# The up products of the feed-forward and gated blocks: 256-column low-weight products alternate with 512-column ones

## What is computed

```python
def conv_glu_ffn(h, w_in, conv_w, conv_b, w_out):      # twice ("ffn")
    gate, val = split(h @ w_in)                        # 1024 -> 2 x 2816
    gate = conv3_along_tokens(gate, conv_w) + conv_b
    return (gelu(gate) * val) @ w_out                  # 2816 -> 1024

def swiglu(x, w_gate, w_up, w_down):                   # twice ("glu")
    return (silu(x @ w_gate) * (x @ w_up)) @ w_down
```

## Time and profile before

| | us |
|---|---|
| median of 3 runs | 1209.4 |
| lowest, highest | 1207.72, 1209.48 |
| the profiled execution, first to last instruction | 1208.0 |
| TensorE busy | 1189.8 (98%) |
| TensorE weight loads | 1038.1 (86%) |
| VectorE busy | 939.8 (78%) |
| ScalarE busy | 667.1 (55%) |
| GpSimd busy | 150.4 (12%) |
| busy share of the DMA queue with the weights | 52.2% |

### The profile page before, as it was taken

How to read it: one execution, slowest core, us unless ns; L and a number is a source line. 1 busy time by engine, 2 the same in 40 slices (tenths; PEclk the granted TensorE clock), 3 DMA queues, 4 the chain that set the end, 5 groups by cost and what they waited for, 6 DMA issues and landing times.

```text
span 1208.0 us, 17902 instructions
## 1 busy us (share of the span) xinstructions
PE 1189.8 (98%) x6979; PEld 1038.1 (86%) x6979; DVE 939.8 (78%) x1270; ACT 667.1 (55%) x1060; POOL 150.4 (12%) x275
## 2 busy tenths in 40 slices
PE   8999999999999999999999999999999999999997
PEld 7898888888889988888888988888897888888886
DVE  6767898888776679989887889777775968667765
ACT  5665654444767776544447755434676555444445
POOL 5300510000200012000002100000208420000002
PEclk9999999999999999999999999999999999999999
DMA  7847386555544445665555565655455146565540
GB/s 245 254 154 232 137 269 209 177 196 170 187 151 150 132 149 200 209 206 178 193 170 185 183 230 182 201 178 170 147 175 174 36 156 211 183 209 184 200 140 36
DMA packets 151640, 215.84 MB, mean 179 GB/s; under 512 B 6970, under 2 KB 116924, under 8 KB 151556
## 3 DMA queue, kind: packets, MB, share of 16 engines
q1 hardware_dynamic: 148092, 207.46, 52.2%
q0 software_dynamic: 1760, 3.94, 1.2%
q10 hardware_dynamic: 1704, 3.28, 0.8%
HBM read 213.60 MB, written 1.06 MB: 178 GB/s over the span
## 4 chain that ended last, share of the span: by engine, by line
PE 91%; DVE 4%; ACT 2%; issue 1%; POOL 1%; DMA 0%; POOLq 0%; ACTq 0%; DVEq 0%
PE work L2408 24%; PE work L2411 13%; PE acc L1996 10%; PE acc L1997 9%; PE acc L1998 9%; PE work L1996 5%; PE work L1998 5%; PE work L1997 5%; DVE w_lo L1298 1%; PE work L2397 1%; PE work L2385 1%; PE work L2399 1%; PE work L2018 1%; PE work L2526 1%; PE acc L2053 1%
## 5 line engine op out<-in xcount | busy, mean ns | idle before, releaser
L1298 DVE TENSOR_TENSOR w_lo<-raw,w_hi 128x2048 fp32r<-128x2048 f32 (+1 forms) x194 | 440.7, 2278 | 60.6 <-ACT w_hi L719 60.6
L719 ACT ACTIVATE w_hi<-raw 128x2048 fp32r<-128x2048 f32 (+2 forms) x193 | 365.2, 1898 | 69.5 <-PE work L2411 60.1
L2408 PE MATMUL work<-hT_both,w_hi 128*128 128x512 f32 x1280 | 318.8, 391 | 0.0
L2408 PEld LDWEIGHTS work<-hT_both,w_hi 128*128 128x128 f32 x1280 | 234.8, 188 | 45.2
L2411 PEld LDWEIGHTS work<-hT_both,w_lo 128*128 128x128 f32 x1280 | 174.6, 190 | 12.5
L2411 PE MATMUL work<-hT_both,w_lo 128*128 128x256 f32 x1280 | 178.5, 282 | 0.0
L1996 PE MATMUL acc<-w_hi,aux_hi 128*128 128x512 f32 x400 | 157.8, 395 | 0.0
L1997 PE MATMUL acc<-w_lo,aux_hi 128*128 128x512 f32 x400 | 156.7, 392 | 0.0
L1998 PE MATMUL acc<-w_hi,aux_lo 128*128 128x512 f32 x400 | 155.8, 390 | 0.0
L1085 ACT ACTIVATE aux_hi<-Z 128x256 fp32r<-128x256 f32 x88 | 36.9, 419 | 195.8 <-DVE Z L1722 107.8
L1693 DVE TENSOR_REDUCE Z<-work 128x256 f32<-128x512 f32 x88 | 60.6, 689 | 90.2 <-PE work L2411 88.5
(11 more groups left out here) (271 smaller groups left out, 1782.4 us busy)
## 6 DMA issues: line engine op xcount, KB each, us to landing
raw<-in_ffn_w_in SPq DMA_DIRECT2D x44, 1024.0 KB, 5.2
raw<-in_ffn_w_out SPq DMA_DIRECT2D x22, 1024.0 KB, 5.0
raw<-in_w_gate SPq DMA_DIRECT2D x22, 1024.0 KB, 5.3
raw<-in_w_up SPq DMA_DIRECT2D x22, 1024.0 KB, 5.3
raw<-in_w_down SPq DMA_DIRECT2D x22, 1024.0 KB, 5.0
raw<-in_na_w_qkv SPq DMA_DIRECT2D x12, 1024.0 KB, 7.5
raw<-in_da_w_qkv SPq DMA_DIRECT2D x12, 1024.0 KB, 5.3
raw<-in_ple_w_gate SPq DMA_DIRECT2D x8, 1024.0 KB, 5.0
```

The lines of the kernel that those rows point to most:

```text
L719: act.activation(w_hi[:, n % RING, 0:size], raw[:, n % RAW, 0:size], ACT.Copy).then_inc(hi_done, 1)
L1298: dve.tensor_tensor(w_lo[:, n % RING, 0:size], raw[:, n % RAW, 0:size], w_hi[:, n % RING, 0:size].bitcast(F32), ALU.subtract).then_inc(lo_ ...
L2408: pe.matmul(b.rearrange("p (e s) -> p e s", e=2), v[0][:, k, cols(c % 2)], hT_both[:, k, :, :], start=k == 0, stop=False)
```

## The change

A constant `LAG = 4` is added and `up` is written anew. The products, their operands and banks are the same, and so are their number and the order of k within a kind. What is new is the order: after four big products of half 0, each further big product is followed by a small one, four steps behind it. The last four small products of half 0 stand between the first four big ones of half 1; the last four of half 1 stand alone at the end. So one call goes: 4 big, 12 pairs of big and small, 4 small. Before a half's first big product the wait is now for `hi_done`; that for `lo_done` comes before the half's first small product. The bank of half 0 is full after half 1's fourth big product, that of half 1 at the end as before.

```diff
--- before.py
+++ after.py
@@ -63,6 +63,7 @@
 N_EARLY = 56
 N_CONV = 3 * FT + FT
 EARLY_UP = FT - 4
+LAG = 4
 RELOAD = 16
 
 
@@ -1997,10 +1998,13 @@
                 pe.matmul(dst, stationary[0], moving[1], start=False, stop=False)
                 return pe.matmul(dst, stationary[1], moving[0], start=False, stop=last)
 
+            def slab_views(n):
+                k, c = slabs[n][1:3]
+                return [r[:, n % RING, 0:k * c].rearrange("p (k n) -> p k n", k=k) for r in (w_hi, w_lo)]
+
             def slab(n):
                 pe.wait_ge(lo_done, n + 1)
-                k, c = slabs[n][1:3]
-                return [r[:, n % RING, 0:k * c].rearrange("p (k n) -> p k n", k=k) for r in (w_hi, w_lo)]
+                return slab_views(n)
 
             def both(pair, *at):
                 return [v[at] for v in pair]
@@ -2400,17 +2404,39 @@
                                             start=False, stop=last)
                             if last:
                                 ins.then_inc(bank_full[(up_bank(ph, c) + i) % WORK], 1)
+                def up_part(ph, c, i, part, k):
+                    g, v = up_bank(ph, c) + i, slab_views(b0 + 3 * (c // 2) - (c >= 2) + i)
+                    d = work[:, g % WORK, :]
+                    if part == 0:
+                        return pe.matmul(d.rearrange("p (e s) -> p e s", e=2), v[0][:, k, cols(c % 2)],
+                                         hT_both[:, k, :, :], start=k == 0, stop=False)
+                    ins = pe.matmul(d[:, 0:S], v[1][:, k, cols(c % 2)], hT_hi[:, k, :], start=False, stop=k == KT - 1)
+                    if k == KT - 1:
+                        ins.then_inc(bank_full[g % WORK], 1)
+                    return ins
+
                 def up(c):
                     g, n = up_bank(ph, c), b0 + 3 * (c // 2) - (c >= 2)
-                    for i in range(2):
-                        v, b = slab(n + i), open_bank(pe, g + i)
-                        for k in range(KT):
-                            pe.matmul(b.rearrange("p (e s) -> p e s", e=2), v[0][:, k, cols(c % 2)], hT_both[:, k, :, :],
-                                      start=k == 0, stop=False)
-                        for k in range(KT):
-                            ins = pe.matmul(b[:, 0:S], v[1][:, k, cols(c % 2)], hT_hi[:, k, :],
-                                            start=False, stop=k == KT - 1)
-                        ins.then_inc(bank_full[(g + i) % WORK], 1)
+                    pe.wait_ge(hi_done, n + 1)
+                    open_bank(pe, g)
+                    for k in range(KT):
+                        up_part(ph, c, 0, 0, k)
+                        if k == LAG:
+                            pe.wait_ge(lo_done, n + 1)
+                        if k >= LAG:
+                            up_part(ph, c, 0, 1, k - LAG)
+                    pe.wait_ge(hi_done, n + 2)
+                    open_bank(pe, g + 1)
+                    for k in range(KT):
+                        up_part(ph, c, 1, 0, k)
+                        if k < LAG:
+                            up_part(ph, c, 0, 1, KT - LAG + k)
+                        if k == LAG:
+                            pe.wait_ge(lo_done, n + 2)
+                        if k >= LAG:
+                            up_part(ph, c, 1, 1, k - LAG)
+                    for k in range(KT - LAG, KT):
+                        up_part(ph, c, 1, 1, k)
 
                 def down(c, ts=range(T)):
                     v = slab(b0 + min(3 * (c // 2) + 4, 3 * STEPS - 1))
```

## The result

The changed kernel takes 1214.0 us (median of 5 runs, 1212.36 to 1214.68) against 1209.48 for the kernel before (5 runs, 1207.72 to 1210.15). The ratio is 1.0041, 95% interval 1.0028 to 1.0053: slower by 4.5 us, where 0.3 us less was forecast (1209.1). The profiled execution spans 1212.1 us, 4.1 more than the 1208.0 of before.

A forecast was written before the change was run, and what follows sets the result against it. TensorE's own pace was taken as the bound; -0.8 us from the order of products and +0.5 us at the ffn block ends gave -0.3 us, 1209.1 us against 1209.4. Own range 1207 to 1211.8, 8 in 10 1202.4 to 1214.9.

The forecast's parts named there:

- What bounds the kernel: Whole kernel: TensorE busy 98% of the span and, inside the wide layers, waiting for nobody.
- Part 1, the pace of the pairs: Order of products in up: a call takes 5.570 us, 0.010 less, times 80 calls -0.8 us.
- P: Time of one big and one small product alternating in up: 0.347 us taken, bounds 0.340 and 0.353 to 0.356.
- its sign of being wrong: In the 12 pairs of a call: P leaving 0.345 to 0.350 us would show the forecast wrong.
- the prediction's own sum: One call of up: 1.406 + 12 P us, including 0.02 that small products leave behind.
- the 5.58 that stands for before: One up in the kernel before: 5.56 us, 5.58 with what it leaves in the down.
- No cover to be had: Weight loads in up: by the skill's rule 107 ns, just fitting behind 256 columns, so alternation has nothing to cover.
- The equal 0.013 us over the columns: Big and small products: both exceed columns at 2.4 GHz by 0.013 us, read as a fixed price of changing weights.
- The loads are covered: Rival, pairs in up: small products take 0.113 us, P = 0.340, -7.0 us in all, 1202.4 us; chance 0.32.
- Part 2, the waits: Separate waits for w_hi and w_lo in up: looser wait gives nothing, earlier need fits 1.95 us lead; 0 us.
- Part 3, the late bank: Gate half's bank full 0.93 us later: 0 mid-block, 0 to 0.25 us per ffn block end, +0.5 us taken for two.
- each change of kind costs: Rival, big product in the 12 pairs: a debt at every change, P = 0.353, 1214.9 us; chance 0.23.

The follow-up runs named there:

- e1: Kernel before with test stretches on TensorE behind the stored result, of one width or mixed; only starts count: 512 with 256 columns one by one took 353 ns a pair.
- e2: Kernel before, its product order kept, with the changed kernel's waits for hi_done and lo_done: 1208.16 us against 1209.42, ratio 0.9994.
- e9: Changed kernel with two big and two small products at a time in place of one and one: 1208.67 us against 1208.02 for the kernel before, ratio 1.0001.
- e4: Kernel before with big and small products alternating within each half, small one step behind, old waits, bank 0 full at its old place: 1213.68 us against 1209.42.
- e3: Kernel before with all 16 big products of a call first, then all 16 small ones: 1210.3 us against 1209.42, ratio 1.0005.
- e6: Kernel before with two big, two small products in turn within each half, old waits: 1208.6 us against 1209.52, ratio 0.9993.
- e7: Kernel before with a second test stretch behind the stored result: more widths, mixtures and group sizes; only starts count: 512 with 272 columns took 360 ns a pair.

## Why the prediction went wrong, point by point

- *What bounds the kernel* was right: TensorE's own pace, no wait. The loss came without one.
- *Part 1, the pace of the pairs* failed, in the value taken between its two bounds. It put P at 0.347 because the first two steps at a change of kind, 0.233 and 0.114, add up to the steady paces, and let every pair repeat these first steps. The trace after has two pairs of three near them (232 with 118, 235 with 114) and one that is not (241 with 120), and the mean is 0.353: the big product's step rose to 0.236, and the small one's fell from 0.120 to 0.117 and not to 0.114. So a small product doesn't gain about as much as the big one loses. P left the 0.345 to 0.350 that the prediction gave as its sign of being wrong. What the rows of before did show is that the big products stay off their best pace for five steps (0.232 each on average), so the first steps could not be taken as the pace of an order that changes all the time. P = 0.353 in the prediction's own sum gives +5.0 us for the calls; the blocks grew by 4.11. With what it leaves in the down a call took 5.640 us, where that sum has 5.642; most of the rest is the rounding of the 5.58 that stands for before, 5.587 by the nanosecond starts.
- *No cover to be had* was right. The equal 0.013 us over the columns holds for both widths (e1), but it isn't fixed: it is 12 to 17 ns over other widths. What settles it is the floor of a product with its load, 0.110 to 0.112, below the 0.120 of a small one. "The loads are covered" is out: no order of 512 with 256 came to 0.340.
- *Part 2, the waits* at 0: right (e2). From the first block on, no wait of TensorE after the change names `w_lo` or `w_hi`.
- *Part 3, the late bank* was right in the middle of the blocks: VectorE's wait rose from 88.5 to 97.2 us and ScalarE's from 60.1 to 73.7, far less than 0.93 us each time, and e9 shows that it costs nothing there. At the ends of the ffn blocks 0 to 0.25 us was said and 0.5 us taken for two; there were 0.12 and 0.10. The bank is their likely cause: e9, which keeps it late, has 0.13 and 0.14 there, and e4, which doesn't, has 0.02 and -0.03. In the changed kernel down(21) comes 0.08 us late in its second product:

```profile
309.19 0.39 PE L1999 MATMUL acc<-w_hi,aux_lo 128*128 128x512 f32 x1
309.42 0.47 PE L1997 MATMUL acc<-w_hi,aux_hi 128*128 128x512 f32 x1
```

  (by the nanosecond starts the next product comes after 307 ns, 80 more than 227). The term was small here, but e3 shows that the same place costs 1.1 us a block once the bank is later still.
- *The rivals*: the slower one, "each change of kind costs", gave 1214.9 and the time was 1214.0, inside the range of 8 in 10 and outside the forecast's own. Its place, the big product in the pairs, was right. Its P of 0.353 is in part luck: it added 0.233 and 0.120, and the trace has 0.236 and 0.117. Its mechanism was wrong: it is not a price on each change (e6 has more changes from small to big in a call than the kernel before, 8 against 2, and is not slower), but the loss of the steady pace in an order that never lets the big products settle.

What stays open is the cause behind the 512-column product's two paces. The runs show that it needs no other engine, no special operand and no bank, and that the order alone decides. They don't show which part of TensorE counts the cycle of three pairs.

## What to carry to other kernels

A steady pace read from a run of equal products holds for such runs alone, and the first steps at a single change of kind don't add up to the pace of an order that changes all the time. If none of the trace's stretches has the order in question, give the bounds equal weight, or put the order into a stretch of its own behind the kernel, which gave the pace to the nanosecond here. Before interleaving to cover weight loads, compare a narrow product's pace with the pace of a still narrower one: if the narrower is faster, the load isn't the bound. When results come later without anyone waiting for them in the middle of a loop, look at the loop's end, where the slack of the other engines is used up.

## What the runs showed of the hardware

- A product with its own weight load has a floor of 0.109 to 0.112 us up to 240 columns (e1, e7), and a wide neighbour doesn't bring a product below it: 512 with 128 columns takes 338 ns a pair (e1), 111 more than the wide one alone, where 128 columns at 2.4 GHz are 53.
- Products of 512 fp32r columns settle at 227 ns only among themselves. Behind a run of 256 columns they take 228 to 236 ns for five steps, one by one with 256 columns 232 to 241, 236 on average. Of 320 to 480 columns mixed with 256, none lost anything (e1, e7).
- The Trainium skill's "TensorE: Matmul & The Clock Gate", section "Back-to-back issue gap", puts the isolated distance at columns / 2.4 + 2.5 ns; for fp32r products with a new load each, from 256 columns up, the test stretches show 12 to 17 ns over columns / 2.4, at the full granted clock.
